# Paged cache loads of a hybrid decoder step: two rows on each of 64 partitions instead of one row on each of 128

## What is computed

```python
PAST_LEN, PAGE_SIZE, DEC_BATCH, B_HEADS, HEAD_DIM = 2048, 128, 8, 4, 64

def diff_attention_rows(q, q_pos, k, v, lam):
    s = jnp.einsum('bqhce,bkhce->bhcqk', q.astype(jnp.float32), k.astype(jnp.float32)) * (e ** -0.5)
    mask = jnp.arange(k.shape[1])[None, :] <= q_pos[:, None]
    a = jax.nn.softmax(jnp.where(mask, s, -jnp.inf), axis=-1)
    attn = a[:, :, 0] - lam * a[:, :, 1]
    return jnp.einsum('bhqk,bkhe->bqhe', attn, v.astype(jnp.float32))

def sample_mixer(...):
    ...
    past_k = pool_k[page_table].reshape(b, PAST_LEN, B_HEADS, 2, HEAD_DIM)
    past_v = pool_v[page_table].reshape(b, PAST_LEN, B_HEADS, B_VDIM)
    ...
```

## Time and profile before

| | us |
|---|---|
| median of 3 runs | 1729.64 |
| lowest and highest | 1726.21, 1733.06 |
| span of the profiled execution | 1722.1 |
| attention, about | 722 to 1160 |
| TensorE busy | 1523.3 (88%) |
| packets of the DMA queue, share of 16 engines | 46.7% |

### The profile page before, as it was taken

How to read it: one execution, slowest core, us unless ns; L and a number is a source line. 1 busy time by engine, 2 the same in 40 slices (tenths; PEclk the granted TensorE clock), 3 DMA queues, 4 the chain that set the end, 5 groups by cost and what they waited for, 6 DMA issues and landing times.

```text
span 1722.1 us, 31526 instructions
## 1 busy us (share of the span) xinstructions
PE 1523.3 (88%) x12377; PEld 1338.7 (78%) x12377; DVE 659.6 (38%) x1293; ACT 511.7 (30%) x829; POOL 66.3 (4%) x156
## 2 busy tenths in 40 slices
PE   4899999989996999788888777778789999989996
PEld 2788999989985767655565555548689999989995
DVE  1222323222235524255555555545542323222224
ACT  2322222211114222234444444442242222221113
POOL 0100000000002000000000000000010000000000
PEclk9899999999998999999999999988889999999998
DMA  9993222222212232379889998772112222232211
GB/s 337 385 310 117 86 75 84 85 84 84 84 53 69 61 129 70 119 215 275 264 265 275 269 251 263 236 215 78 50 49 86 85 74 85 85 91 68 84 50 55
DMA packets 212310, 245.52 MB, mean 143 GB/s; under 512 B 8511, under 2 KB 152377, under 8 KB 209154
## 3 DMA queue, kind: packets, MB, share of 16 engines
q1 hardware_dynamic: 212226, 244.42, 46.7%
HBM read 237.31 MB, written 7.08 MB: 142 GB/s over the span
## 4 chain that ended last, share of the span: by engine, by line
PE 77%; DVE 6%; DMA 5%; SPq 5%; issue 3%; ACT 3%; ACTq 0%; DVEq 0%
PE ps L273 53%; PE ps L769 10%; DMA kv<-in_cache_diff_k_dram 3%; SPq L975 2%; PE ps L1111 2%; PE ps L1058 2%; SPq L955 2%; PE ps L1070 2%; PE ps L558 2%; PE ps L381 2%; PE ps L1154 2%; DMA wada<-in_w_ada_dram 1%; DVE PP L1287 1%; PE ps L1129 1%; DVE KC L1279 1%
## 5 line engine op out<-in xcount | busy, mean ns | idle before, releaser
L252 ACT ACTIVATE whi<-w 128x1024 fp32r<-128x1024 f32 (+1 forms) x152 | 171.1, 1129 | 801.4 <-PE ps L273 687.1
L258 DVE TENSOR_TENSOR wlo<-w,whi 128x1024 fp32r<-128x1024 f32 (+1 forms) x152 | 200.0, 1318 | 412.3 <-ACT whi L252 411.9
L273 PE MATMUL ps<-hhi,whi 128*128 128x288 f32 x1536 | 332.9, 298 | 19.0 <-DVE hlo L311 13.6
L273 PE MATMUL ps<-hlo,whi 128*128 128x288 f32 x1536 | 330.7, 297 | 0.0
L273 PE MATMUL ps<-hhi,wlo 128*128 128x288 f32 x1536 | 330.2, 297 | 0.0
L273 PEld LDWEIGHTS ps<-hhi,whi 128*128 128x128 f32 x1536 | 249.1, 190 | 26.3 <-DVE hlo L311 14.0
L273 PEld LDWEIGHTS ps<-hlo,whi 128*128 128x128 f32 x1536 | 249.5, 190 | 0.0
L273 PEld LDWEIGHTS ps<-hhi,wlo 128*128 128x128 f32 x1536 | 249.2, 190 | 0.0
L273 PE MATMUL ps<-ffhi,whi 128*128 128x288 f32 x704 | 152.8, 299 | 9.2 <-DVE wlo L258 9.2
L1058 PEld LDWEIGHTS ps<-ident,kv 128*128 128x128 f32 (+1 forms) x896 | 98.6, 146 | 77.5 <-issue 59.1
L1058 PE MATMUL ps<-ident,kv 128*128 128x128 f32 (+1 forms) x896 | 122.4, 278 | 35.3 <-DMA kv<-in_cache_diff_k_dram 19.1
(11 more groups left out here) (158 smaller groups left out, 1585.0 us busy)
## 6 DMA issues: line engine op xcount, KB each, us to landing
w<-in_ffn_w_in_dram SPq DMA_DIRECT2D x88, 512.0 KB, 3.9
wada<-in_w_ada_dram SPq DMA_DIRECT2D x18, 2048.0 KB, 12.4
kv<-in_cache_diff_k_dram SPq DMA_DIRECT2D x128, 256.0 KB, 5.1
kv<-in_cache_diff_v_dram SPq DMA_DIRECT2D x128, 256.0 KB, 3.6
w<-in_ffn_w_out_dram SPq DMA_DIRECT2D x32, 704.0 KB, 4.6
w<-in_w_qkv_dram SPq DMA_DIRECT2D x24, 512.0 KB, 3.7
kv<-in_cache_win_k_dram SPq DMA_DIRECT2D x16, 768.0 KB, 6.1
kv<-in_cache_win_v_dram SPq DMA_DIRECT2D x16, 768.0 KB, 9.0
```

The lines of the kernel that those rows point to most:

```text
L252: nc.scalar.activation(whi[:, slot, 0:w], w32[:, slot, 0:w], ACT.Copy).then_inc(ph.hi, 1)
L258: nc.vector.tensor_tensor(wlo[:, slot, 0:w], w32[:, slot, 0:w], whi[:, slot, 0:w].bitcast(F32), ALU.subtract).then_inc(ph.lo, 1)
L273: m = pe.matmul(ps[:, banks + h, 0:TH], w, x[:, kk, h * TH:(h + 1) * TH], start=(kk == 0 and n == 0), stop=(kk == kall - 1 and n == 2))
```

## The change

Only the DMA of a page is written in another way. The page is seen as 64 pairs of rows, and each pair (2 x 2 KB, contiguous in the chip's memory) goes to one partition, into two neighbouring tiles. Pages k = 0 and 2 of a quarter go to partitions 0 to 63, pages 1 and 3 to partitions 64 to 127; pages 0 and 1 fill tiles 0 and 1, pages 2 and 3 tiles 2 and 3. The number of DMAs, their 256 KB, their order, and all waits and semaphores stay. The keys of a sequence come in another order, and the values in the same one.

```diff
                 else:
                     for k in range(n):
-                        src = pool[is_v][ds(page[k], 1), :, :].rearrange("a p c -> (a p) c")
-                        eng.dma_start(slot[:, k, :], src).then_inc(s, 16)
+                        src = pool[is_v][ds(page[k], 1), :, :].rearrange("a (p t) c -> (a p) t c", t=2)
+                        rows_k, tiles_k = slice(k % 2 * (P // 2), (k % 2 + 1) * (P // 2)), slice(k // 2 * 2, k // 2 * 2 + 2)
+                        eng.dma_start(slot[rows_k, tiles_k, :], src).then_inc(s, 16)
```

## The result

The changed kernel takes 1767.55 us (median of four runs, 1753.81 to 1777.88), the kernel before 1729.74 us. The ratio is 1.022, 95% interval 1.018 to 1.026: slower by 38 us, where 1782 us was forecast. The profiled execution has a span of 1764.2 us, 42.1 us more than before.

The account below looks back on a forecast made before the run. SyncE's pace, TensorE's quarter and at times transfers alternate as the bound; slower page loads fill the DMA engines. Stretches add +40.5, +7.4, +3.9, +1, together +52.8 us: span 1774.9, plus 7.5 gives 1782 us; range 1728 to 1835.

Parts of the forecast that it names:

- the full level: Attention stage: the DMA busy share at which the engines count as full, taken as 0.97.
- the page packets: Attention page loads: a 4 KB packet to 64 partitions takes 305 ns, a load 4.88 us, +1.36 us a load.
- the last stretch: Attention, 1100 to 1156 us, nine page loads: 54.1 us needed of 56 us, +1 us for local collisions.
- the one load of the same shape: Start of the trace: the sample input, 64 packets of 4 KB to partitions 0 to 63, read as 293 ns each.
- half of a delay: Page packets in the attention: 24 ns more than in a quiet store; 305 ns is the middle of 293 and 317.
- rival 1: Attention page loads: the two halves run side by side, no change, 1729 up to 1745 us; chance 0.18.
- The point from which I let it decide: Attention page loads: up to 244 ns a packet, 3.90 us a load, the engines' slack means nothing is lost.
- rows 8 and 9: Trace stretches of 4 KB packets: to 128 partitions at 162 ns, and the sample input to 64 at 293 ns.
- The busy time: Attention, five middle sequences: engines busy 232.1 us plus 54.5 us from page loads, 286.6 us in all.
- SyncE's issues: Page issues on SyncE: left at 0.333 us each, change taken as zero, bounded as a gain of 0 to 5.3 us a sequence.
- What I put around the span: Whole kernel: 7.5 us by which the median of the runs is above the profiled span, added to 1774.9 us.
- Rival 2 (faster): Attention page loads: slowness comes from memory rows, not 64 partitions; a load costs 3.0 us, time 1720 us; chance 0.08.

Follow-up runs that it names:

- e4: The changed kernel with pages on every second partition (even or odd), so 64 partitions reach over all 128: 1749.8 us, ratio 1.012 to the kernel before.
- e6: The changed kernel without alternation, pages 0 and 1 in the lower half, 2 and 3 in the upper: 1796.54 us, ratio 1.040 to the kernel before.
- e1: The kernel before with one more, unused page-number read on SyncE ahead of each load of four pages: 1749.15 us, ratio 1.013.
- e2: The changed kernel with three page numbers read per load, third page loaded twice, fourth not at all: 1768.05 us, ratio 1.022 to the kernel before.
- e7: The kernel before with the new page form for key pages only, value pages as before: 1754.21 us, ratio 1.016.
- e5: e4 with three page numbers read per load, third page loaded twice, fourth not at all: 1736.59 us, ratio 1.007 to the kernel before.

## Why the prediction was right, point by point

The mechanism came out as forecast: a page to one half of the partitions takes more of the engines' time, the engines are full, and the stage grows. Several sizes inside the sum were off: the full level, the page packets, the last stretch. The page packets that I took too long were made good by a cost that I had left out; that part is luck.

**Packets to one half are slow: right, and a little smaller than taken.** I took 305 ns from the one load of the same shape plus half of a delay. The changed kernel has 247 to 278 ns where pages alone move and about 276 over the middle; e4 shows that the half, not the 64 rows or the 4 KB, is the cause, and e6 speaks for what made it smaller: without alternation it is 284 to 302 ns, near the 293 of the single load and the 305 I took. What I gave as rival 1, engines apart by a page, is real in part. It was not enough to hide the cost. The point from which I let it decide (244 ns) fits what was found: the change is above it and its engines are full, e4 is about at it or below (201 to 247 ns) and they are not.

**How full the engines get: wrong by 4 to 5 points.** I took 0.97 from ten us of queued transfers, and had 1.007 and 1.03 in rows 8 and 9. The changed kernel has 1.01 over five sequences. With 1.01 in the place of 0.97, and all else as it was, the five sequences come out at 286.6 / 1.01 = 283.8 us, +28.8, and measured is +29.0. So this term makes up for the 11.5 us by which the five sequences were forecast too long.

**The busy time: right as a sum, not in its parts.** The engines were busy 1.01 x 286.6 = 289.5 us in the five sequences, for the 286.6 I had summed up (that both figures are 286.6 is chance: one is busy time, the other the measured length). But I had all of the +54.5 us from the pages. By the packet records in the order of issue, pages are at 278 ns there, which is +41 us for the 40 loads, and the 512 KB window loads, whose form is untouched and which I had left as they were, go from 189 to about 256 ns a packet: (20 x 128 x 67 ns) / 16 = +11 us. So by this estimate slow transfers also slow the others on the same engines. The forecast left that out, and the page packets that it took too long made good for it.

**SyncE's issues: wrong.** I said zero and bounded it below nothing, as a gain. They take 136 ns more each. The trace hinted at it: the load to 64 partitions was issued in 0.58 us, next to 0.40, and I used that pair to argue only that fewer packets don't shorten an issue. That pair is no clean measure, since the second issue follows directly on the first, and what goes before changes an issue's length too (last section). The stores of the prompt's and the samples' values, 128 partitions and 64, stand alone and say it plainly in the timeline of the kernel before:

```profile
716.54 0.34 SPq L713 DMA_DIRECT2D out_dram<-V  x1
...
722.02 0.47 SPq L713 DMA_DIRECT2D out_dram<-V  x1
```

Had I priced it as 0.54 us a load, I would have had e1's loss, 1.3%, as a second way to slower. It changed nothing in the sum, since the two costs are limits side by side and the larger one sets the time (e2); it would have changed rival 1, which, with quick packets, is not "no change" but e4: 1.012.

**The last stretch: wrong.** I used a share of 0.72 averaged over 56 us and found room. From the last sequence's first page issue to the end of the loads it was 52.6 us (1104.2 to 1156.8) and is 59.5 us, +6.9 us for my +1. Of these, 6.3 us are in its first part, up to the 16 last page issues, which themselves went from 19.04 to 19.66 us. The first part before and after:

```profile
1104.20:1137.60 33.40, 26.42 (x345) 18.44 (x349) 20.13 (x59) 18.11 (x39) 1.49 (x4) 1.00 0.79 236
...
1144.30:1184.00 39.70, 28.30 (x345) 19.64 (x349) 20.36 (x59) 17.86 (x39) 1.48 (x4) 0.96 0.86 207
```

The engines had room there on average, 0.79, and it still grew by 19%. So a mean share below 1.0 does not hide longer transfers; e7 fits that, with a share of 0.91 before in the middle sequences. Which of its waits grew is not followed up here.

**The sum, by stretch.** First sequence +6.2 us (forecast +7.4), five in the middle +29.0 (+40.5), the seventh +2.3 (+3.9), the last +6.9 (+1): together +44.4 us (+52.8). The rest of the kernel became some 2 us shorter. What I put around the span was too much as well: the profiled execution of the changed kernel has a device time of 1765.99 us for its span of 1764.2, 1.8 us and not 7.5; the other 5.7 us were spread between runs. The median is 3.4 us above that span.

**Rival 2 (faster)** fell with e4 and e5: the packets of 4 KB that reach over all partitions take no less time for their bytes than those of 2 KB before (212 against 2 x 107 ns), the slow issues come with the form, and with SyncE's pace of before the ratio is still 1.007.

## What to carry to other kernels

In these runs a transfer that touches only the lower or the upper half of the partitions took more engine time, with packets of 2 KB and of 4 KB: 1.8 times as much for one load by itself (293 against 162 ns), 1.3 times with halves that alternate in a busy stage, against 64 partitions spread over all 128 (276 against 212 ns). A mean share of 0.8 or 0.9 on the DMA engines was no protection from it. Before trusting that larger packets help, look for a transfer of the same shape elsewhere in the trace, and read all of its row: the duration of its issue as well as that of its packets. Count the transfers beside it too, since they slow down with it. Engine time and issue pace did not add here (1.3% for the pace alone, 2.2% with and without it once the packets are slow); find which one is next, as e2 and e4 do, before summing them.

## What the runs showed of the hardware

- The duration of an issue on SyncE depends on its form: for a page it is 333 ns to 128 partitions with one run each, 469 ns to 64 neighbouring partitions, 475 ns to 64 partitions in steps of two, and 599 ns to 64 partitions with two runs each. It also depends on the issue just before it. The window loads of L967 are the same in both kernels. Right behind page issues they take 428 ns before (first row) and 582 ns after (second row), and 318 ns after where they stand by themselves (third row; ns min/median/max):

```profile
L967 SPq DMA_DIRECT2D kv<-in_cache_win_v_dram x16: 419/428/441, 749.9 to 1119.5; - x16
...
L967 SPq DMA_DIRECT2D kv<-in_cache_win_v_dram x16: 572/582/591, 753.6 to 1162.4; - x16
...
L967 SPq DMA_DIRECT2D kv<-in_cache_win_k_dram x16: 312/318/518, 725.1 to 1123.4; - x16
```

- 64 partitions in steps of two take packets of 4 KB in 201 to 247 ns (about 212 over the middle), 64 neighbouring ones in 247 to 278 ns with alternating halves (276) and 284 to 302 ns without (304). The Trainium skill, "SBUF — State Buffer", section on Door 1, the DMA port swizzle, has it that what counts is how many of the 16 ports the partitions reach, and by that rule steps of two reach all of them; e4 agrees, with a share of 0.83 for 1.01 at about the same GB/s, though no trace shows the ports themselves. The Trainium skill, "DMA: Bandwidth & Descriptors", section "Rules for kernel authors", has two transfers to disjoint halves serialize; e6 against the changed kernel (284 to 302 against 247 to 278 ns) speaks for an overlap in part when both halves are queued.
- One DMA after another to alternating halves is 1.8% quicker for the whole kernel than two and two (1.040 against 1.022).
